# Expert layer: eleven row buffers in place of twelve

## The reference

```python
def peer_ffn(hn, w_pq, sub_keys, u_tab, v_tab):
    ...
    best_s, best_c = lax.top_k(cand.reshape(T, PEER_HEADS, K * K), K)
    ...
    expert = ia * PEER_N_KEYS + ib
    gate = jax.nn.softmax(best_s, axis=-1)
    ...
    def token_block(args):
        xb, eb, gb = args
        a = jnp.einsum('td,ted->te', xb, u_tab[eb])
        hidden = gb.astype(xb.dtype) * jax.nn.gelu(a)
        return jnp.einsum('te,ted->td', hidden, v_tab[eb])
```

## Time and profile before

| | |
|---|---|
| time, median of 3 runs | 3106.89 us (3106.46 to 3109.78) |
| the profiled execution: its time | 3108.23 us |
| the profiled execution: its span | 3106.4 us |
| busy share of the span: PE, DVE, ACT, POOL | 88%, 68%, 37%, 32% |
| rows gathered from `u` and `v` (line 1289) | 256 and 256, median 14.7 and 14.8 us from issue to landing |
| dense rows (line 1284) | 32, median 15.0 us from issue to landing |

### The profile page before, as it was taken

How to read it: one execution, slowest core, us unless ns; L and a number is a source line. 1 busy time by engine, 2 the same in 40 slices (tenths; PEclk the granted TensorE clock), 3 DMA queues, 4 the chain that set the end, 5 groups by cost and what they waited for, 6 DMA issues and landing times.

```text
span 3106.4 us, 34641 instructions
## 1 busy us (share of the span) xinstructions
PE 2728.9 (88%) x12196; PEld 1978.6 (64%) x12196; DVE 2112.7 (68%) x2869; ACT 1146.9 (37%) x1980; POOL 981.4 (32%) x566
## 2 busy tenths in 40 slices
PE   8999999999999999999999994676667786769997
PEld 8888788888887888999779891222223332235433
DVE  5687665555564555445555679788788887779877
ACT  5455655555553335445665540000002330034000
POOL 0011000000000000000000027877777877778864
PEclk9999999999999999989999997889898988888999
DMA  6444445555555554443345469999999999999997
GB/s 264 148 161 163 175 178 188 187 189 186 190 187 184 189 188 170 163 163 136 136 164 178 162 234 387 414 415 413 409 417 398 418 413 406 407 383 378 406 412 302
DMA packets 123586, 827.89 MB, mean 267 GB/s; under 512 B 22167, under 2 KB 22183, under 8 KB 23855
## 3 DMA queue, kind: packets, MB, share of 16 engines
q0 software_dynamic: 79392, 510.36, 40.6%
q1 hardware_dynamic: 43920, 313.73, 27.8%
q10 hardware_dynamic: 144, 2.10, 0.2%
HBM read 892.00 MB, written 4.22 MB: 289 GB/s over the span
## 4 chain that ended last, share of the span: by engine, by line
PE 18%; POOL 13%; DMA 10%; DVE 9%; issue 4%; ACT 3%; DVEq 0%; ACTq 0%
POOL rows L1289 13%; PE ps L598 12%; DMA rows<-peer_u,arena 6%; DVE arena L2388 3%; DMA rows<-peer_v 2%; PE ps L1196 2%; PE ps L1207 1%; DMA rows<-peer_v,arena 1%; ACT arena L1750 1%; PE ps L1187 1%; DVE arena L209 1%; DVE arena L202 0%; DVE arena L203 0%; DVE arena L206 0%; DVE arena L199 0%
## 5 line engine op out<-in xcount | busy, mean ns | idle before, releaser
L503 DVE SCALAR_TENSOR_TENSOR WL<-ring,PA,WH 128x512 fp32r<-128x512 f32 x896 | 633.6, 753 | 474.4 <-ACT WH L486 458.6
L1207 PE MATMUL ps<-rows,rstd 128*128 128x512 f32 x1164 | 631.6, 696 | 302.5 <-DMA rows<-peer_v,arena 213.4
L2388 DVE CUSTOM_DVE_ANT_0 arena<-rows,arena 128x2048 f32<-128x2048 f32 x256 | 586.9, 2293 | 146.1 <-DMA rows<-peer_u,arena 118.5
L1207 PEld LDWEIGHTS ps<-rows,rstd 128*128 128x128 f32 x1164 | 246.9, 222 | 674.2 <-issue 380.8
L1289 POOL DMA_INDIRECT rows<-peer_v,arena x256 | 491.7, 1921 | 199.5 <-DVE arena L2388 77.2
L485 ACT ACTIVATE WH<-ring,PA 128x512 fp32r<-128x512 f32 x448 | 324.3, 724 | 552.2 <-PE ps L598 405.3
L1289 POOL DMA_INDIRECT rows<-peer_u,arena x256 | 437.6, 1709 | 167.3 <-DVE WL L503 79.8
L598 PE MATMUL ps<-WH,HH 128*128 128x512 f32 x1120 | 442.3, 395 | 4.3 <-DVE WL L503 4.3
L598 PE MATMUL ps<-WH,HL 128*128 128x512 f32 x1120 | 437.6, 391 | 0.0
L598 PE MATMUL ps<-WL,HH 128*128 128x512 f32 x1120 | 437.3, 390 | 0.0
L598 PE MATMUL ps<-HH,WH 128*128 128x256 f32 x1088 | 312.7, 287 | 17.7 <-DVE WL L503 17.7
(11 more groups left out here) (361 smaller groups left out, 3549.7 us busy)
## 6 DMA issues: line engine op xcount, KB each, us to landing
ring<-stream SPq DMA_DIRECT2D x292, 1024.0 KB, 4.8
rows<-peer_v POOLq DMA_DIRECT2D x32, 1024.0 KB, 15.0
rows<-peer_u,arena POOLq DMA_INDIRECT x256, 14.7
rows<-peer_v,arena POOLq DMA_INDIRECT x256, 14.8
arena<-xT SPq DMA_DIRECT2D x4, 512.0 KB, 8.9
bias_rows<-bias_scratch POOLq DMA_DIRECT2D x1, 2048.0 KB, 10.4
arena<-xT ACTq DMA_DIRECT2D x1, 2048.0 KB, 9.7
arena<-memT POOLq DMA_DIRECT2D x1, 2048.0 KB, 9.1
```

The source lines that it names most:

```text
L503: ins = nc.vector.scalar_tensor_tensor(out=half_tile(WL, u)[:, s], in0=raw_half(u)[:, s], scalar=gain[d], in1=half_tile(WH, u).bitcast(f32 ...
L1207: last = mm(ps[:, 4 * tt + q, :], DIAG[:, k % DIAGS, :], rows[:, SLOTS[n % ROWS], q * CH:(q + 1) * CH], start=n == mine[0], stop=n == ends[q])
L2388: ins = V.tensor_tensor_reduce(out=JUNK, in0=rows[:, SLOTS[n % ROWS], :], in1=HN[:, tt, :], scale=1.0, scalar=0.0, op0=ALU.mult, op1=ALU.a ...
```

## The change

The number of row buffers goes from 12 to 11. The last place, `11`, drops out of `SLOTS`, and every `n % ROWS` now counts modulo 11.

```diff
-ROWS = 12
+ROWS = 11
 GROUPS = TT * PEER_H
 EARLY = 2
-SLOTS = [0, 1, 2, 3, 8, 10, 4, 6, 5, 7, 9, 11]
+SLOTS = [0, 1, 2, 3, 8, 10, 4, 6, 5, 7, 9]
```

## The result

| | before | eleven buffers |
|---|---|---|
| time, median of 20 runs | 3106.16 us (3101.42 to 3114.79) | 3113.19 us (3108.71 to 3117.66) |
| ratio, with its 95% interval | | 1.0023 (1.0017 to 1.0029) |
| span of the profiled execution | 3106.4 us | 3109.4 us |

The kernel became 0.23% slower, 7.0 us; the interval is 5.3 to 9.0 us. The range of 3107 to 3117 us holds the median. Single executions of one kernel scatter by some 10 us here, so that the two spans alone (3.0 us apart) say little; the traces are compared place by place.

What follows compares the result with a forecast made beforehand. The prediction took the DMA engines to bound the expert layer; 2.4 us at the first `choose` and 2.2 us at row 407 sum to +4.6 us over 3106.89 us, 3111.5 us, range 3107.0 to 3117.0 us.

Steps and rivals of the forecast that it cites:

- the two dry places: POOL's long waits at row 32 and row 407, where the DMA queue runs dry; a slot lost at each, +4.6 us.
- rival 2: The wait for PE's late dense gates also loses a slot: +2.4 us more, 3113.9 us; chance 0.10.
- The first `choose`: Row 31 takes over row 32's wait for DVE with the queue already dry: +2.4 us (1.3 to 3.3).
- Row 407: Row 406 takes over its 8.84 us wait for PE's line 1207, queue dry: +2.2 us (1.7 to 2.9).
- The later waits on line 2388: Twelve POOL waits for DVE after later chooses; queued rows (4.5 or 2.7 us at least) cover the slot: 0.
- the dense part: 19 POOL waits on PE's line 1196; the last 46 rows have 8.8 us in reserve: 0.
- the reserve: A row's time from issue to landing above 7.2 us, the landing into an empty queue; a slot within it costs nothing.
- Row 233: Waits for PE's late dense gates; row 232 takes over, one slot just uses up 2.4 us: 0, at most 2.4.
- Rival 1: Both dry queues are refilled at no loss, so nothing is lost: 3107 us; chance 0.15.
- Rivals 3 and 4: Every later `choose` costs a slot, 3141 us; or every dense-part wait loses one, 3152 us; chance 0.05 each.
- rival 3: Each of the 12 later waits on line 2388 costs 2.44 us, 29 us more: 3141 us; chance 0.05.

Runs made afterwards that it cites:

- the two waits alone: Kernel before, twelve buffers, with two waits added: row 31 for row 20 and row 406 for row 395; ratio 1.0012 (1.0004 to 1.0021), +3.7 us.
- full rows: Kernel before with gathered `v` rows leaving out no token, with twelve and with eleven buffers: 1.0377 and 1.0384, medians 3220.67 and 3224.95 us.

## Why the prediction was right, and where it was short

- *The DMA engines bound the expert layer, and a buffer less costs only where the queue is empty*: right for the two dry places. The wait of two rows alone costs 3.7 us, the same wait on more than 500 other rows 3.4 us. "Empty" has to be said of each of the 16 DMA engines, though, and the prediction said it of all together.
- *The number*: the loss of 4.6 us was too small, below the interval of 5.3 to 9.0 us. The range held the measured time because its upper end had been widened for rival 2 and for scatter; the loss that filled it came from elsewhere, so that is luck in part. The likeliest outcome that I named, within 0.2% of before (0.70), did not come: it is 0.23% (0.17 to 0.29), for which I had 0.27.
- *The first `choose`, +2.4 us*: right in place and in size. Row 33 was issued one slot of 2.45 us later (1917.89 + 2.20 against 1917.63), and the DMA pause is one stretch longer; the rows behind it landed 1.9 us later here and 2.5 us later with the two waits alone.
- *Row 407, +2.2 us*: right. The landings on its two sides moved by 2.7 and then 5.2 us; with the two waits alone the same stretch lost 2.1 us. The expectation of a low DMA share that lasts 2 us longer there did not come true.
- *The later waits on line 2388 and the dense part, 0*: this is the step that failed in size. It measured 3.4 us (0.6 to 6.2). The error was in the reserve: I took a row's landing time less 7.2 us for the reserve of all DMA engines, but a landing is set by the slowest of them, and the first report was near that of an empty queue all along. What of the 3.4 us lies behind the chooses and what in the dense part no run separated; in the traces the dense part lost nothing with eleven and with ten buffers, and with ten the loss lies between rows 44 and 388.
- *Row 233*: rival 2, a loss of one more slot there. No run tried the place alone. In the trace with eleven buffers row 232 did not have to wait for PE, and the landings from row 225 to row 240 kept their delay (4.1 and 4.2 us), so that the loss is not there in that execution. That rival 2's figure of 7.0 us is what was measured is chance.
- *Rival 1* (nothing lost) is out, since the interval of the change begins at 5.3 us. *Rivals 3 and 4* are out for eleven buffers; with nine and eight the chooses do begin to cost, up to rival 3's price. The rule of the Trainium skill beside rival 3, "SBUF — State Buffer", section "SBUF: two separate sides", is about DMA engines that sit idle because GpSimd is kept from writing descriptors. Here an issue takes 2.14 us beside DVE's line 2388 and 0.99 us otherwise; what the longer issues cost, apart from the waits for a buffer, no run shows.
- That uneven loads of the DMA engines make the loss outside the two places is supported and not settled. Row 306's reports show DMA engines that ran dry beside two that had not, and with full rows no dips are left. But full rows also deepened the queue, and the difference in time (4.3 against 7.0 us) is within the intervals.

## What to carry to other kernels

A pool of buffers in front of a saturated DMA queue is a reserve of time. A buffer less costs nothing where, at the end of every wait, rows are still queued, and its full slot where the queue is already dry; find those places first, as two of them made about half of the loss here. Read the reserve from the mean DMA share in short stretches behind a wait as well as from the time to landing, because the latter follows the slowest DMA engine. And the first buffers given up say little about the next: 7, 12, 33 and 38 us.

## What was not expected of the hardware

With rows that leave out tokens, a mean DMA share of 0.68 stood beside a row that took 14.3 us to land; with full rows the DMA share had no dip under 0.95 for 780 us, and the stream ran at 422 GB/s from 1960 to 2360 us instead of 414. Leaving out 68 MB of 570 saved 117 us, and not the 164 us that those bytes take at 414 GB/s.
